# A two-block transformer kernel: latents' norms in halves, index scores ahead of the first chunk's rows, mixing ahead on GpSimd

## The reference

```python
mod = silu(c) @ ada_w + ada_b                       # 6 x 1024 modulation values
h = rms_norm(x, mix_pre_norm) * (1 + sc_m) + sh_m
proj = h @ w_in                                     # 456 latent columns, then 1824 for the recurrence
c_q, c_kv, idx_k_raw, idx_w_raw = split(att_p, ...) # 256, 128, 64, 8
cq, ckv, ik = rms_norm(c_q), rms_norm(c_kv), rms_norm(idx_k_raw)
iq = einsum('btr,rhd->bthd', cq, w_idx_q)
# per query: score over all earlier positions, the best 256 are kept
score = einsum('bth,bths->bts', iw, relu(einsum('bthd,bsd->bths', iq, ik)))
_, sel = top_k(where(causal, score, -inf), 256)
# softmax over the selected keys, with rel_bias[t5_bucket(t - s)] added
# beside it a recurrence over time, heads of 64:
p = p + mu_shift * (p_prev - p)                     # mixing with the token before
r, k, v, wd, ad, gd = split(p, ...)                 # 512, 512, 512, 64, 64, 160
S = S * w_t + (S @ a_t) b_t^T + v_t k_t^T;  y_t = S @ r_t
mix = concat([y_att, y_rwkv]) @ w_out               # then feed-forward, then block two
```

## Time and profile before

| | |
|---|---|
| median of three runs | 3649.11 us |
| profiled execution | 3646.83 us, its span 3645.5 us |
| PE busy | 3346.4 us, 92% of the span |
| DVE busy | 1794.3 us, 49% |
| ACT busy | 928.1 us, 25% |
| POOL busy | 339.0 us, 9% |
| granted TensorE clock, mean | 0.962 |

### The profile page before, as it was taken

One profiled execution on the slowest core, in us unless ns is written; L12 is line 12 of the kernel. 1 busy time (PEld: TensorE's weight loads), 2 busy tenths in 40 slices (PEclk: granted clock), 3 DMA queues, 4 the chain that ended last, 5 costly groups with the idle time before them and its releaser, 6 DMA issues.

```text
span 3645.5 us, 51038 instructions
## 1 busy us (share of the span) xinstructions
PE 3346.4 (92%) x21635; PEld 2602.0 (71%) x21650; DVE 1794.3 (49%) x2850; ACT 928.1 (25%) x1709; POOL 339.0 (9%) x278
## 2 busy tenths in 40 slices
PE   7988867887888999999999889999998999999998
PEld 6736655775567788888886556876676888878876
DVE  2378677664556322224545546321246444444656
ACT  2255432333534100001222544000025111111122
POOL 0000245762001000000000000000000000000000
PEclk9989977999999999999999999999999999999999
DMA  6337210101114111113331001111133111123434
GB/s 216 70 65 239 84 42 19 37 20 59 47 64 133 52 47 52 47 47 104 121 118 50 4 24 40 42 35 35 58 116 110 47 47 52 47 75 98 140 115 144
DMA packets 217381, 270.18 MB, mean 74 GB/s; under 512 B 11229, under 2 KB 176387, under 8 KB 216900
## 3 DMA queue, kind: packets, MB, share of 16 engines
q1 hardware_dynamic: 211851, 247.87, 21.3%
q10 hardware_dynamic: 3192, 11.17, 1.7%
q0 software_dynamic: 2112, 7.87, 0.6%
HBM read 232.80 MB, written 34.08 MB: 73 GB/s over the span
## 4 chain that ended last, share of the span: by engine, by line
PE 81%; DVE 11%; ACT 4%; issue 2%; DMA 1%; POOL 1%; SPq 0%; DVEq 0%; ACTq 0%; POOLq 0%
PE psum L2071 18%; PE psum L2073 18%; PE psum L2075 18%; PE psum L523 5%; PE psum L3089 3%; PE psum L1266 2%; PE psum L2589 2%; PE psum L2910 2%; PE psum L2797 2%; PE psum L651 1%; PE psum L1821 1%; PE psum L2926 1%; DVE Lg L1915 1%; PE psum L1847 1%; DMA slot<-in_ada_w 1%
## 5 line engine op out<-in xcount | busy, mean ns | idle before, releaser
L2071 PE MATMUL psum<-hT_hi,wcut_lo 128*128 128x512 f32 x1856 | 589.4, 395 | 16.7 <-DVE hT_lo L2110 16.7
L2073 PE MATMUL psum<-hT_hi,wcut_hi 128*128 128x512 f32 x1856 | 582.8, 391 | 0.0
L2075 PE MATMUL psum<-hT_lo,wcut_hi 128*128 128x512 f32 x1856 | 582.5, 391 | 0.0
L2071 PEld LDWEIGHTS psum<-hT_hi,wcut_lo 128*128 128x128 f32 x1856 | 350.4, 189 | 97.0 <-DVE hT_lo L2110 17.9
L2053 DVE CAST wcut_hi<-raw 128x1024 fp32r<-128x1024 f32 x256 | 176.9, 691 | 478.6 <-PE psum L2075 454.0
L2075 PEld LDWEIGHTS psum<-hT_lo,wcut_hi 128*128 128x128 f32 x1856 | 350.3, 189 | 73.2
L2073 PEld LDWEIGHTS psum<-hT_hi,wcut_hi 128*128 128x128 f32 x1856 | 350.3, 189 | 72.6
L2071 PE MATMUL psum<-wcut_hi,xcut_lo 128*128 128x512 f32 x1120 | 348.7, 393 | 17.6 <-DVE xcut_lo L2189 13.8
L2073 PE MATMUL psum<-wcut_hi,xcut_hi 128*128 128x512 f32 x1120 | 347.2, 392 | 0.0
L2075 PE MATMUL psum<-wcut_lo,xcut_hi 128*128 128x512 f32 x1120 | 346.9, 391 | 0.0
L1097 POOL TENSOR_TENSOR st<-st,nhalf 128x1 f32<-128x1 f32 (+2 forms) x78 | 61.1, 790 | 2827.2 <-DVE st L709 2827.2
(11 more groups left out here) (428 smaller groups left out, 4354.5 us busy)
## 6 DMA issues: line engine op xcount, KB each, us to landing
raw<-in_w_ffn_down SPq DMA_DIRECT2D x88, 512.0 KB, 3.6
raw<-in_w_ffn_up SPq DMA_DIRECT2D x66, 512.0 KB, 3.8
slot<-in_ada_w SPq DMA_DIRECT2D x24, 1024.0 KB, 11.7
raw<-in_w_in SPq DMA_DIRECT2D x28, 512.0 KB, 5.4
raw<-in_w_ffn_gate SPq DMA_DIRECT2D x22, 512.0 KB, 3.9
slot<-in_w_in SPq DMA_DIRECT2D x8, 1024.0 KB, 6.1
raw<-in_w_out SPq DMA_DIRECT2D x16, 512.0 KB, 3.7
x_one<-xrow SPq DMA_DIRECT2D x16, 512.0 KB, 2.8
```

Of the source, the lines that this page charges most:

```text
L2071: pe.matmul(outs[i], al, bs[i][0], start=start, stop=False, skip_group_check=True)
L2073: pe.matmul(outs[i], ah, bs[i][0], start=False, stop=False, skip_group_check=True)
L2075: mm = pe.matmul(outs[i], ah, bs[i][1], start=False, stop=stop, skip_group_check=True)
```

## The change

- The latents' norms are made in two halves of four tiles (`norms_vector`, three parts each): the first half between VectorE's copies of the `att` tiles 4 to 6, the second behind the last. The three powers of a half are one POOL instruction.
- `LAT_STEPS` now holds chunk 0's row steps: five of them, then the turns in pairs with a row step between, then the four queries. The scores follow at once. Chunk 1 is wholly in `ROW_STEPS`, which all engines now begin behind the loras.
- The bias products, their copies and their store move behind the loras too, ahead of row step 0. The waits for that store move from `rwkv_weights` to the first load into `prev` and the first write of `sig`.
- `ROW_STEPS` spreads the 16 modulations as two per three row steps. `ROW_LOADS` and `SLOT_OF` change with it. `rwkv_weights` comes in SP's queue behind modulation (3,2); the store of the latents is taken out of it and comes behind `("rkv", 2)`.
- `passes_beside` gives four passes behind a row step except where a front round stands; 210 of the 223 passes now come ahead of the recurrence, 170 before. `best_steps` gives two per round.
- POOL does a tile's mixing (`keys_pool`) one round earlier, behind the values of the tile before, and tile 0's values and tile 1's mixing ahead of tile 0's first `free` round. ScalarE does front rounds 5 and 6 of tile 0 ahead of its sums of that step.

```diff
-ROW_LOADS = [...] + ["att a", "att b", ("rkv", 0), "idx q", ("rkv", 1), "lora a", "lora b",
+ROW_LOADS = [...] + ["att a", "att b", ("rkv", 0), "idx q", "lora a", "lora b", ("rkv", 1),
...
-LAT_STEPS = [("turn", t) for t in range(NT)] + [("iq", q) for q in range(4)]
+LAT_STEPS = [("rkv", 0, t) for t in range(5)] + [("turn", 0), ("turn", 1), ("rkv", 0, 5), ("turn", 2), ("turn", 3), ("rkv", 0, 6),
+             ("turn", 4), ("turn", 5), ("rkv", 0, 7), ("turn", 6), ("turn", 7)] + [("iq", q) for q in range(4)]
+    LAT_BANK.append((6, 7, 0, 1)[_n[1] % 4] if _row else 2 + 2 * (_n[0] % 2))
...
-        if (1, 5) <= (_c, _t) < (3, 5):
+        if _c < 4 and (8 * _c - 8 + _t) % 3:
...
-SLOT_OF = {_s: (1, 3, 4)[_i % 3] for _i, _s in enumerate(_mods)}
-SLOT_OF.update({("rkv", _c): 2 * (_c % 2) for _c in range(2, 6)})
+SLOT_OF = {_s: 1 + _i % 3 for _i, _s in enumerate(_mods)}
+SLOT_OF.update({("rkv", _c): 4 * (_c % 2) for _c in range(1, 6)})
...
@@ proj_sync
-        if key == ("rkv", 4):
+        if key == ("rkv", 2):
+            latents_store(sp, K)
+        if key == MODS[10]:
             rwkv_weights(sp, K)
@@ proj_tensor: behind the loras
+    pe.wait_ge(*D["hot"].at("hot"))
+    for i, o in enumerate(range(0, 1152, 512)):
+        n = min(512, 1152 - o)
+        pe.wait_ge(*B.free(2 * i))
+        mm = pe.matmul(bank(K, 2 * i)[0:8, 0:n], K.relb[0:33, :], K.oh[0:33, o:o + n], start=True, stop=True, skip_group_check=True)
+        B.until(2 * i, S, ("bias", i))
+    mm.then_inc(*T.up("bias"))
+    for i in range(len(ROW_STEPS) + 1):
@@ proj_vector
     for t in range(NT):
         v.wait_ge(*T.at(("att", 0, t)))
         v.tensor_copy(K.att[:, t, 0:256], ...)
+        if 4 <= t < 7:
+            norms_vector(v, K, 0, t - 4)
+    for part in range(3):
+        norms_vector(v, K, 1, part)
@@ passes_beside
-    return 4 if ROW_STEPS[i - 1][0] == "rkv" and i <= BESIDE else 2
+    return 4 if i and ROW_STEPS[i - 1][0] == "rkv" and round_beside(i) is None else 2
@@ proj_scalar: behind the loras
+    s.wait_ge(*T.at("bias"))
+    for i, o in enumerate(range(0, 1152, 512)):
+        n = min(512, 1152 - o)
+        s.activation(K.oh[0:8, o:o + n], bank(K, 2 * i)[0:8, 0:n], ACT.Copy).then_inc(*S.up(("bias", i)))
+    s.wait_ge(*S.own())
+    s.dma_start(K.vbd.ap(), K.oh[0:8, :].unsqueeze(1).to_broadcast([8, 128, 1152])).then_inc(*D["bias"].up("bias", 16))
+    for i in range(len(ROW_STEPS) + 1):
+        j = round_beside(i)
         if i < len(ROW_STEPS):
             row_scalar(s, K, ROW_STEPS[i], ROW_BANK[i])
+        if j is not None and j >= 5:
+            front_scalar(s, K, 0, j)
         for _ in range(passes_beside(i)):
             next(K.sums, None)
+        if j is not None and j < 5:
+            front_scalar(s, K, 0, j)
@@ best_steps
-    return 3 if g < 14 else 2
+    return 2
@@ recurrence
-VALUES, VALUES_FIRST = 6, 8
+VALUES, VALUES_FIRST = 6, 7
+def keys_pool(g, K, t):
+    g.wait_ge(*K.D["raw"].at(t))
+    g.tensor_tensor(K.prev, K.prev, K.mx, SUB).then_inc(*G.up())
+    g.wait_ge(*G.own())
+    g.tensor_tensor(K.prev, K.prev, K.muB, MUL).then_inc(*G.up(("mixed", t)))
@@ front_pool
+    if t and j == VALUES and t + 1 < NT:
+        keys_pool(g, K, t + 1)
@@ proj_pool, at round_beside(i) == 5
+                keys_pool(g, K, 1)
```

More of the change, by code:

```diff
@@ L290, in layout @@
     K.top = region(W1 - 48, W1).take("top", 8, 6)
+    K.sqs3 = [region(a, a + 4 * n).take("squares", 4, n) for a, n in ((K.P3, 256), (K.P3 + 1024, 128), (K.P3 + 1536, 64))]
     K.lprev, K.ikk = K.rl[0], K.rl[1].rearrange("p (t n) -> p t n", t=8)
@@ L566, in proj_tensor @@
     T.mark(("free", "att b"))
[L567 to L587, removed]
+    for step, b in zip(LAT_STEPS, LAT_BANK):
+        lat_tensor(pe, K, step, b)
     for n, (t, q) in enumerate(SCORES):
@@ L661, in lat_tensor @@
     T, V, S, B = K.T, K.V, K.S, K.bank
+    if step[0] == "rkv":
+        return row_tensor(pe, K, step, b)
     p = bank(K, b, 2)
@@ L666, in lat_tensor @@
         t = step[1]
+        if t == 0:
+            pe.wait_ge(*V.at("latents"))
         pe.transpose(p[:, 0:128], K.att[:, t, 0:128], K.ident)
@@ L762, in proj_vector @@
         v.tensor_copy(K.att[:, t, 0:256], bank(K, 2 + 2 * t % 6)[:, 0:256]).then_inc(*V.up(("att", 0, t)))
[L764 to L784, removed]
+        if 4 <= t < 7:
+            norms_vector(v, K, 0, t - 4)
+    for part in range(3):
+        norms_vector(v, K, 1, part)
+    V.mark("latents")
+    for step, b in zip(LAT_STEPS, LAT_BANK):
+        lat_vector(v, K, step, b)
     for t, q in SCORES:
@@ L792, in proj_vector @@
             next(K.best)
-    for i in range(ROWS_FIRST, len(ROW_STEPS) + 1):
-        if i == ROWS_FIRST + 4:
+    for i in range(len(ROW_STEPS) + 1):
+        if i == 4:
             for m in (1, 2):
@@ L942, in lat_vector @@
     T, V, S = K.T, K.V, K.S
+    if step[0] == "rkv":
+        return
     p = bank(K, b, 2)
@@ L1013, in proj_scalar @@
         s.activation(K.att[:, t, 256:456], bank(K, 2 + (2 * t + 1) % 6)[:, 0:200], ACT.Copy).then_inc(*S.up(("att", 1, t)))
-    for t in range(NT):
-        s.wait_ge(*T.at(("rkv", 0, t)))
-        s.activation(K.stage[1][:, t, :], bank(K, 2 + (4 + t) % 6)[:, 0:256], ACT.Copy).then_inc(*S.up(("rkv", 0, t)))
-    s.wait_ge(*T.at("bias"))
-    for i, o in enumerate(range(0, 1152, 512)):
-        n = min(512, 1152 - o)
-        s.activation(K.oh[0:8, o:o + n], bank(K, 2 + i)[0:8, 0:n], ACT.Copy).then_inc(*S.up(("bias", i)))
-    s.wait_ge(*S.own())
-    s.dma_start(K.vbd.ap(), K.oh[0:8, :].unsqueeze(1).to_broadcast([8, 128, 1152])).then_inc(*D["bias"].up("bias", 16))
-    for i, step in enumerate(LAT_STEPS):
-        lat_scalar(s, K, step, 2 + 2 * (i % 2))
-        if i % 2:
-            row_scalar(s, K, ROW_STEPS[i // 2], ROW_BANK[i // 2])
+    for step, b in zip(LAT_STEPS, LAT_BANK):
+        lat_scalar(s, K, step, b)
     for n, (t, q) in enumerate(SCORES):
@@ L1062, in lat_scalar @@
     T, V, S = K.T, K.V, K.S
+    if step[0] == "rkv":
+        return row_scalar(s, K, step, b)
     p = bank(K, b, 2)
@@ L1192, in rwkv_rows @@
     sp.wait_ge(*D["prows"].at("zero row"))
+    sp.wait_ge(*D["bias"].at("bias"))
     keys_load(sp, K, 0)
@@ L1662, in front_pool @@
     prev, mx, vt = K.prev, K.mx, K.vb[t % 4]
-    if j == 0:
+    if t == 0 and j == 0:
         g.wait_ge(*D["mu"].at("mu"))
-        g.wait_ge(*D["raw"].at(t))
-        g.tensor_tensor(prev, prev, mx, SUB).then_inc(*G.up())
-        g.wait_ge(*G.own())
-        g.tensor_tensor(prev, prev, K.muB, MUL).then_inc(*G.up(("mixed", t)))
+        keys_pool(g, K, 0)
     if j == (VALUES if t else VALUES_FIRST):
```

84 lines of the change are left out of this document (59 added, 25 removed).

## The result

Eleven runs of each kernel: before 3648.99 us (median), after 3666.59. The ratio is 1.0049, 95% interval 1.0029 to 1.0068: the change makes the kernel slower, by about 18 us. The forecast was 3647, "no difference" its likeliest case; 3666.6 lies inside the wide range (3585 to 3678) and outside the likeliest case's own (3631 to 3664). The profiled execution has a span of 3666.0 us, 20.5 above that of before.

The account below looks back on a forecast made before the run. TensorE was taken to fill the rows stage, with nothing full in the recurrence, whose first periods VectorE's search stretched. From 3646.83 us, +54 (to tile 0's mask), -53 (recurrence) and -1 (POOL) gave 3647 us; range 3585 to 3678.

Parts of the forecast that it names:

- likeliest case: Whole kernel: load stalled by the bias store, search mostly off the recurrence; 3647 us, own range 3631 to 3664, chance 0.56.
- Scores: Start of the index scores on TensorE: at 146.0 us, 23.7 us earlier than before.
- Start of the rows stage: Behind the last lora: TensorE stands some 9 us, 4 worse than before, plus 2.5 us of slow clock.
- The store: Rows stage: the 4.6 MB bias store delays modulation (3,3)'s weights to 346 us, stalling TensorE 68 us.
- rival 1: Rows stage: loads pass the store in short turns or on other engines, no 68 us stall; 3576 us, chance 0.22.
- From there to the recurrence: From the stall's end to tile 0's mask: 148.5 + 2 + 1.6 us, mask at 498, +54 us against before.
- "2 us" of VectorE lag: Late rows stage: search and front rounds make VectorE add 2 us before tile 0's mask, bounds 0 and 17.
- rival 2: Rows stage, steps 41 to 56: packed search makes VectorE the bound, 17 us longer; 3665 us, chance 0.22.
- TensorE's wait for `aT`: Before the recurrence: the old 5.32 us wait goes, since ScalarE does these copies ahead of its sums.
- The recurrence: Periods 1 to 4: less search makes them 47, 36, 40 and 44.5 us, sum 167.5 against 220.8, -53 us.
- wait for `vrow`: Period 1: the 10.95 us wait before the first tile product goes, as its inputs are ready earlier.
- POOL's mixing: Later recurrence periods: mixing one round earlier costs a tile product 1 us inside slack; 0 to -1 us in all.

Follow-up runs that it names:

- after_fewer: The changed kernel with 2 instead of 4 search passes beside the row steps from step 50 on; 3664 us.
- pool_order: The changed kernel with POOL's mixing and tile 0's values put back where they were before the change; 3678 us.
- early_fewer_one: The changed kernel with bias work and store before the index scores, 2 search passes from row step 50, one per recurrence round; 3586 us.
- after_fewer_pool: The changed kernel with 2 search passes from row step 50 and POOL's mixing in its old order; 3675 us (one execution).

## Why the prediction was wrong, step by step

- **Scores:** 146.74 for 146.0, no new wait. Right. The last lora ended at some 235 us, 3 to 4 earlier than said.
- **Start of the rows stage:** 9.5 us of waits for 9; it began at 246.7 for 249.9.
- **The store:** the deciding step was right. Stall 69.65 for 68, landing just before 343.95 for 346, one packet for one packet; rival 1 (the loads pass the store) is dead. The sizes came from a row of the same store; the reason I gave for them, eight full engines, is half of it: with eight rows 18 partitions apart, and a share that stays under eight engines' too, a packet takes a quarter of the time.
- **From there to the recurrence: the step that failed first.** 164.6 us for 152.1. The "2 us" of VectorE lag, out of bounds 0 to 17, was 7.3 to 7.8, as each of the two cures measures it. This is rival 2, "search packed into steps 41 to 56 makes VectorE the bound there", and it came about for 7.8 of its 17 us (after_fewer, pool_order). I had argued that waits shrink when VectorE is late; what I left out is that the change puts POOL's mixing and tile 0's values beside exactly these passes, and five of them are stretched by it (2.52 and 2.59 us above, 2.11, 1.64 and 1.44 behind them). Another 4.93 us are TensorE's wait for `aT`, which I had struck out: ScalarE does the copy ahead of the sums of its own step, but still behind those of the step before, which wait for VectorE. Some 2 of the 12.5 us stay unexplained.
- **The recurrence: the second.** -42.4 for -53. Period 1 took 53.6 for 47, outside my 43 to 50. The wait for `vrow` did go (-11), but something else took all of it, where I had added 4 net. The passes' busy time isn't it: 28.2 us for the 13, at the top of my 22 to 28, and 25.1 for before's 21 (I had said 17). What I had wrong is that they would lie partly in VectorE's gaps. VectorE works its list in order, and TensorE's waits for it in period 1, the one for the mask left out, went from 4.0 us before to 21.1, the longest for `TX` behind the widest tile's passes, two of them beside POOL's mixing (kernel after, TensorE, then VectorE):

```profile
551.82 1.97 PE L1297 MATMUL psum<-TX,XX 64*64 64x64 f32 x32 [8.72 <-DVE TX L1383]
```

```profile
548.34 2.73 DVE L950 TENSOR_SCALAR tied<-scores,top 128x1024 bf16<-128x1024 f32 x1
551.00 0.68 DVE L1383 TENSOR_TENSOR TX<-psum,mk 128x512 f32<-128x512 f32 x1
551.71 3.72 DVE L953 TENSOR_TENSOR_SCAN rank<-tied,top 128x1024 f32<-128x1024 bf16 x1
```

With 7 narrower passes instead of the 13 these waits are 8.8 us and the period is 17 us shorter (early_fewer_one). Periods 2 to 4 took 37.7, 41.2 and 45.9 for 36, 40 and 44.5, all inside their bounds: that search was what stretched them is shown by period 2 and 3 moving with the passes (37.4 to 44.0, 41.2 to 49.8).
- **POOL's mixing:** 0 to -1 forecast. Counted from the end of the stall to mask 7, undoing the whole reordering of POOL changes -0.5 us (pool_order), and costs 10.5 once VectorE isn't late for mask 0 (after_fewer_pool against after_fewer). Nearly all of that is in periods 1 and 2 (8.3 and 2.4 us). From period 5 on they are 44.3 to 45.1 us in all four kernels.
- **Sum:** +54 - 53 - 1 became +64.2 - 42.4 (POOL's part is in both) - 1.4 behind mask 7. Two terms of 50 were each off by 10 us to the same side. 3665, rival 2's price, is the number that came, for half of its reason; I gave that case 0.22.

## What to carry to other kernels

Moving a large transfer moves what it collides with: here one store behind the loras cost 75 us at mask 7 and buried a reordering worth 53. Ask of a store which partitions it reads, not only how many bytes it has. And when the engine that does filler work is given more of it ahead of a deadline, count what the neighbour engine does in the same microseconds; where two large terms cancel, the forecast is as wide as both.

## What the runs showed of the hardware that I had not expected

- A packet of 4.6 KB takes 0.70, 0.30, 0.18 or 0.18 us by which partitions it is read from, with eight source rows in the first three (above).
- Two queues that share an engine alternate row by row, 4.6 KB against 1 KB: a 1 MB load landed after 77.1 us.
- A two-input VectorE instruction waits out POOL's running one: 2.06 us for 6 numbers. So do some passes with one tensor (2.73 us for 0.75).
- Behind mask 7 the 14 profiled executions fall into two groups, 2845.9 to 2847.5 us (eight) and 2856.2 to 2859.1 (six); no edit touches that part. Stretches some 50 and 70 us behind mask 7, the kernel after, then pool_order (busy times; granted clock third from the end):

```profile
869.93:879.93 10.00, 9.28 (x146) 5.60 (x142) 5.69 (x10) 1.92 (x4) 4.97 (x4) 1.00 0.91 304
889.93:899.93 10.00, 10.00 (x22) 4.29 (x21) 2.77 (x4) 2.07 (x4) 0.00 (x0) 0.88 0.31 105
```

```profile
872.24:882.24 10.00, 10.00 (x101) 6.50 (x99) 3.87 (x7) 0.60 (x1) 3.23 (x3) 0.50 1.00 342
892.24:902.24 10.00, 4.92 (x9) 2.49 (x10) 1.61 (x3) 0.60 (x1) 2.52 (x2) 0.50 0.28 97
```

From 50 to 60 us behind mask 7 the granted clock is 1.00 in all eight of the first group and 0.50 in all six of the second: TensorE runs there at 1.2 instead of 2.4 GHz. The kernels' own runs spread by as much (before: 3640 to 3661). What decides it isn't settled; it is why effects under 10 us are read from the masks here.
